# Seven block products for slabs of a feed-forward's first matrices, squares on ScalarE

## The reference

```python
def squared_relu_mlp(x, w1, w2):
    return jnp.square(jax.nn.relu(x @ w1)) @ w2      # w1: 1024 x 4096, w2: 4096 x 1024, DEPTH = 2 layers

for i in range(DEPTH):
    ...                                              # mix = attention (i = 0) or state space (i = 1)
    x = layer_norm(DN_ALPHA * x + mix, ...)
    x = layer_norm(DN_ALPHA * x + squared_relu_mlp(x, mlp_w1[i], mlp_w2[i]), ...)
```

## Time and profile before

| | us |
|---|---|
| median of three runs (lowest, highest) | 2304.91 (2304.09, 2306.13) |
| the profiled execution, whole | 2307.19 |
| its span, first to last instruction | 2305.3 |
| TensorE busy in it | 2272.6 |
| VectorE busy | 979.7 |
| ScalarE busy | 444.2 |
| mean granted TensorE clock, share of full | 0.995 |

### The profile page before, as it was taken

One profiled execution on the slowest core, in us unless ns is written; L12 is line 12 of the kernel. 1 busy time (PEld: TensorE's weight loads), 2 busy tenths in 40 slices (PEclk: granted clock), 3 DMA queues, 4 the chain that ended last, 5 costly groups with the idle time before them and its releaser, 6 DMA issues.

```text
span 2305.3 us, 25572 instructions
## 1 busy us (share of the span) xinstructions
PE 2272.6 (99%) x10790; PEld 1369.9 (59%) x10790; DVE 979.7 (42%) x1950; ACT 444.2 (19%) x1011; POOL 73.9 (3%) x130
## 2 busy tenths in 40 slices
PE   9999999999999999999999999999999999999998
PEld 6568547886487459997434333335999643333332
DVE  3567656667576557653211111125774311111122
ACT  3410003357100011220211111101132121111111
POOL 2000000000100000000000000000000000000000
PEclk9999999999999999999999999999999999999999
DMA  7289625354698415246999999994426599999997
GB/s 292 114 309 403 252 78 204 147 183 180 238 403 328 178 65 197 97 182 256 390 427 427 428 427 428 428 418 185 164 97 247 222 407 428 428 427 428 427 428 286
DMA packets 59167, 671.64 MB, mean 291 GB/s; under 512 B 7504, under 2 KB 7792, under 8 KB 18720
## 3 DMA queue, kind: packets, MB, share of 16 engines
q1 hardware_dynamic: 51888, 649.45, 69.0%
q0 software_dynamic: 7152, 20.43, 2.6%
HBM read 666.59 MB, written 3.26 MB: 291 GB/s over the span
## 4 chain that ended last, share of the span: by engine, by line
PE 87%; DMA 9%; DVE 2%; issue 0%; ACT 0%; SPq 0%; POOL 0%; DVEq 0%; POOLq 0%; ACTq 0%
PE ps L101 85%; DMA ring<-in_exp_w 5%; DMA arena<-in_exp_w 3%; DVE arena L114 1%; PE ps L349 1%; DVE arena L117 1%; PE ps L2753 1%; DMA arena<-ssm_rows 1%; DMA ring<-in_ada_w 0%; PE ps L638 0%; DMA ring<-in_attn_w_in 0%; PE ps L1915 0%; DVE X L117 0%; PE ps L1234 0%; ACT arena L106 0%
## 5 line engine op out<-in xcount | busy, mean ns | idle before, releaser
L101 PE MATMUL ps<-arena 128*64 128x512 f32 (+8 forms) x4036 | 957.3, 466 | 15.1 <-DMA arena<-in_exp_w 6.0
L101 PEld LDWEIGHTS ps<-arena 128*128 128x128 f32 (+2 forms) x4036 | 462.2, 167 | 466.1 <-issue 436.6
L101 PE MATMUL ps<-ring,arena 128*64 128x512 f32 (+2 forms) x1720 | 460.6, 584 | 1.9 <-DMA ring<-in_exp_w 1.9
L101 PE MATMUL ps<-XTGB,ring 128*128 128x256 f32 (+1 forms) x2160 | 423.5, 353 | 0.0
L101 PEld LDWEIGHTS ps<-XTGB,ring 128*128 128x128 f32 x2160 | 367.1, 190 | 52.8 <-issue 10.7
L101 PEld LDWEIGHTS ps<-ring,arena 128*64 128x64 f32 (+1 forms) x1720 | 174.0, 150 | 259.0 <-issue 254.5
L122 DVE COPY arena<-ps 128x512 f32<-128x512 f32 (+5 forms) x133 | 63.3, 496 | 417.4 <-PE ps L101 298.5
L121 ACT COPY arena<-ps 128x512 f32<-128x512 f32 (+3 forms) x179 | 81.6, 475 | 677.9 <-PE ps L2753 285.1
L101 PE MATMUL ps<-XTGB,arena 128*64 128x512 f32 (+2 forms) x736 | 200.7, 428 | 0.0
L105 ACT ACTIVATE arena<-ps 128x512 f32<-128x512 f32 (+2 forms) x95 | 51.2, 545 | 677.1 <-PE ps L101 672.3
L101 PE MATMUL ps<-ring,XTGB 128*128 128x512 f32 (+3 forms) x484 | 169.1, 504 | 2.0 <-DMA ring<-in_attn_w_in 1.9
(11 more groups left out here) (151 smaller groups left out, 950.8 us busy)
## 6 DMA issues: line engine op xcount, KB each, us to landing
arena<-in_exp_w SPq DMA_DIRECT2D x90, 2048.0 KB, 26.6
ring<-in_exp_w SPq DMA_DIRECT2D x68, 2048.0 KB, 28.0
ring<-in_mlp_w SPq DMA_DIRECT2D x25, 2048.0 KB, 9.7
ring<-in_ada_w SPq DMA_DIRECT2D x20, 2048.0 KB, 9.8
XTGB<-in_exp_w SPq DMA_DIRECT2D x18, 2048.0 KB, 32.3
ring<-in_ssm_w_in SPq DMA_DIRECT2D x12, 2048.0 KB, 7.7
ring<-in_w_in SPq DMA_DIRECT2D x12, 2048.0 KB, 8.0
ring<-in_gate_w SPq DMA_DIRECT2D x12, 2048.0 KB, 7.6
```

Of the source, the lines that this page charges most:

```text
L101: return self.e.matmul(o, lhsT=lhsT, rhs=rhs, start=start, stop=stop, skip_group_check=True)
```

## The change

For slabs 2 and 4 of layer 0 and 2, 4 and 6 of layer 1 the product with w1 is made by seven block products instead of eight. `w1_x_sums` makes four sums of blocks of `XT` once a layer on VectorE, `w1_sums` four sums of weight blocks for each such slab (one of them in place in the slab), `w1_products` issues the products (7 x 2 column blocks x 4 chunks, 128 columns each) into four banks, and `w1_results` adds them up from PSUM into `hT` in seven VectorE instructions; ScalarE copies the first product. ScalarE then takes relu and square of the whole slab. For all other slabs of 1 to 7 the square, too, moves from VectorE to ScalarE, right after the relu. VectorE's program in `mlp_dve` is put in a new order, with the sums for slab s + 2 ahead of the pieces of step s and the results of slab s + 1 behind them. `W1_LOADS` and `PIECES` stay as they are. New buffers `hX`, `hS` lie in the arena.

```diff
--- before.py
+++ after.py
@@ -873,6 +873,78 @@
         ORDER = (1, 2, 3, 5, 7, 6, 4), (1, 5, 6, 2, 3, 7, 4)
         PLAIN = {2: 0, 3: 1, 4: 2}
 
+        W1_BLOCKS = (2, 4), (2, 4, 6)
+        W1_GROUPS = ((1, 6), (5, 7), (3, 4), (2,))
+
+        def w1_x_sums(v, l, nn):
+
+            x1, x2, x3, x4 = hX[l]
+            v.wait_ge(at("XT", nn, 0), at("XT", nn, 1))
+            k = v.then_inc(v.tt(x1, XT[:, 0:4, P:T], XT[:, 0:4, 0:P], ALU.subtract), ("hX", l))
+            v.then_inc(v.tt(x3, XT[:, 4:8, P:T], XT[:, 0:4, P:T], ALU.subtract), ("hX", l))
+            v.wait_ge(k)
+            k = v.then_inc(v.tt(x2, XT[:, 4:8, P:T], x1, ALU.subtract), ("hX", l))
+            v.wait_ge(k)
+            v.then_inc(v.tt(x4, XT[:, 4:8, 0:P], x2, ALU.subtract), ("hX", l))
+
+        def w1_sums(v, l, s):
+
+            w = weights(("m1", l, s))
+            s1, s2, s4 = hS[l]
+            v.wait_ge(at("w", ("m1", l, s)), at("hp", l, s - 2, 2) if s > 2 else None)
+            k = v.then_inc(v.tt(s1, w[:, 0:4, T:2 * T], w[:, 4:8, T:2 * T], ALU.add), ("hS", l, s, 5))
+            v.wait_ge(k)
+            k = v.then_inc(v.tt(s2, s1, w[:, 0:4, 0:T], ALU.subtract), ("hS", l, s, 6))
+            v.then_inc(v.tt(w[:, 0:4, T:2 * T], w[:, 0:4, 0:T], w[:, 0:4, T:2 * T], ALU.subtract), ("hS", l, s, 7))
+            v.wait_ge(k)
+            v.then_inc(v.tt(s4, w[:, 4:8, 0:T], s2, ALU.subtract), ("hS", l, s, 3))
+
+        def w1_products(pe, l, s):
+            slab_ = ("m1", l, s)
+            w = weights(slab_)
+            x1, x2, x3, x4 = hX[l]
+            s1, s2, s4 = hS[l]
+            pairs = {1: (XT[:, 0:4, 0:P], w[:, 0:4, 0:T]), 2: (XT[:, 4:8, 0:P], w[:, 4:8, 0:T]), 3: (XT[:, 4:8, P:T], s4),
+                     4: (x4, w[:, 4:8, T:2 * T]), 5: (x1, s1), 6: (x2, s2), 7: (x3, w[:, 0:4, T:2 * T])}
+            pe.wait_ge(at("w", slab_), at("hX", l))
+            for r, group in enumerate(W1_GROUPS):
+                ps = bank(pe, "hp", l, s, r)
+                for n, p in enumerate(group):
+                    x, y = pairs[p]
+                    if p in (3, 5, 6, 7):
+                        pe.wait_ge(at("hS", l, s, p))
+                    for f in range(2):
+                        for c in range(4):
+                            ins = pe.mm(ps[:, n * T + f * P:n * T + (f + 1) * P], y[:, c, f * P:(f + 1) * P], x[:, c, :],
+                                        c == 0, c == 3)
+                pe.then_inc(ins, ("hp", l, s, r), *([("free", slab_)] if r == 3 else []))
+
+        def w1_product(l, s, r, n):
+            return ps_of("hp", l, s, r)[:, n * T:(n + 1) * T].rearrange("p (f t) -> p f t", f=2)
+
+        def w1_parts(hT, s):
+            g = hT[:, 4 * s:4 * s + 4, :]
+            return g[:, 0:2, 0:P], g[:, 0:2, P:T], g[:, 2:4, 0:P], g[:, 2:4, P:T]
+
+        def w1_results(v, l, s, hT):
+            c11, c12, c21, c22 = w1_parts(hT, s)
+
+            def plus(o, r, n, x, *done):
+                return v.then_inc(v.tt(o, w1_product(l, s, r, n), x, ALU.add), ("read", "hp", l, s, r), *done)
+
+            v.wait_ge(at("hp", l, s, 0), at("hP1", l, s))
+            k = plus(c12, 0, 1, c11)
+            v.wait_ge(k, at("hp", l, s, 1))
+            k = plus(c21, 1, 1, c12)
+            e = plus(c12, 1, 0, c12)
+            v.wait_ge(k)
+            k = plus(c22, 1, 0, c21, ("hsum", l, s))
+            v.wait_ge(k, e, at("hp", l, s, 2))
+            plus(c12, 2, 0, c12, ("hsum", l, s))
+            plus(c21, 2, 1, c21, ("hsum", l, s))
+            v.wait_ge(at("hp", l, s, 3))
+            plus(c11, 3, 0, c11, ("hsum", l, s))
+
         def blocks_a(hT, s):
             return [hT[:, 4 * s + 2 * k:4 * s + 2 * k + 2, t * P:(t + 1) * P] for t in range(2) for k in range(2)]
 
@@ -914,7 +986,10 @@
                                 mid=None if t else lambda: turn_rows(pe, n, 1, X, at("x", n, 1)))
                 else:
                     ada_pe(pe, l, s, acc)
-                    gemm_f(pe, ("m1", l, s), ("m1", l, s), 4, mid=(lambda: ada_pe(pe, l, 8, acc)) if s == 7 else None)
+                    if s in W1_BLOCKS[l]:
+                        w1_products(pe, l, s)
+                    else:
+                        gemm_f(pe, ("m1", l, s), ("m1", l, s), 4, mid=(lambda: ada_pe(pe, l, 8, acc)) if s == 7 else None)
                 if s == 1:
                     for t in range(2):
                         turn(pe, ("h0", l), t, lambda c: h0[:, t, c * P:(c + 1) * P], 4, at("relu 0", l, t))
@@ -965,10 +1040,21 @@
                 act.then_inc(act.act(h0[:, t, :], ps_of("m1", l, 0, t), ACT.Relu), ("relu 0", l, t),
                              ("read", "m1", l, 0, t))
             for s in range(1, 8):
+                if s in W1_BLOCKS[l]:
+                    act.wait_ge(at("hp", l, s, 0))
+                    act.then_inc(act.cp(w1_parts(hT, s)[0], w1_product(l, s, 0, 0)), ("hP1", l, s), ("read", "hp", l, s, 0))
+                    h = hT[:, 4 * s:4 * s + 4, :]
+                    act.wait_ge(at("hsum", l, s))
+                    k = act.then_inc(act.act(h, h, ACT.Relu))
+                    act.wait_ge(k)
+                    act.then_inc(act.act(h, h, ACT.Square), ("h", l, s))
+                    continue
                 for fp in range(2):
+                    h = hT[:, 4 * s + 2 * fp:4 * s + 2 * fp + 2, :]
                     act.wait_ge(at("m1", l, s, fp))
-                    act.then_inc(act.act(hT[:, 4 * s + 2 * fp:4 * s + 2 * fp + 2, :], two(ps_of("m1", l, s, fp)),
-                                         ACT.Relu), ("relu", l, s, fp), ("read", "m1", l, s, fp))
+                    k = act.then_inc(act.act(h, two(ps_of("m1", l, s, fp)), ACT.Relu), ("read", "m1", l, s, fp))
+                    act.wait_ge(k)
+                    act.then_inc(act.act(h, h, ACT.Square), ("h", l, s))
                 if s == 1:
                     for t in range(2):
                         act.wait_ge(at("h0", l, t, 0))
@@ -1040,18 +1126,18 @@
                 norm_v(v, n, 1, rest)
 
         def mlp_dve(v, l, hT, acc, ab, sA, sB):
+            w1_x_sums(v, l, 1 + 2 * l)
             for s in range(8):
-                if s == 7:
-                    ada_dve(v, l, s, acc, ab)
-                    block_sums(v, l, 0, hT, sA, sB)
-                for fp in range(2 if s else 0):
-                    h = hT[:, 4 * s + 2 * fp:4 * s + 2 * fp + 2, :]
-                    v.wait_ge(at("relu", l, s, fp))
-                    v.then_inc(v.tt(h, h, h, ALU.mult), ("h", l, s))
-                if s < 7:
-                    if l and s == 1:
-                        gain_dve(v, 0)
-                    ada_dve(v, l, s, acc, ab)
+                if l and s == 1:
+                    gain_dve(v, 0)
+                if s and s + 2 in W1_BLOCKS[l]:
+                    w1_sums(v, l, s + 2)
+                ada_dve(v, l, s, acc, ab)
+                if s == 0:
+                    w1_sums(v, l, 2)
+                if s + 1 in W1_BLOCKS[l]:
+                    w1_results(v, l, s + 1, hT)
+            block_sums(v, l, 0, hT, sA, sB)
             for s in range(1, NS):
                 block_sums(v, l, s, hT, sA, sB)
 
@@ -1072,6 +1158,9 @@
         h00 = arena.get(2, 512)
         sU0 = arena.get(512)
         sA0, sB0 = strassen_places(acc_at, h0_at, ab_at)
+        hX, hS = [None, None], [None, None]
+        hX[0] = [arena.get(4, P) for _ in range(4)]
+        hS[0] = [arena.get(4, T) for _ in range(3)]
 
 
 
@@ -1556,6 +1645,11 @@
         sU1 = arena.get(512)
         assert arena.pos <= TOP + SLAB
         sA1, sB1 = strassen_places(acc_at, h0_at, ab_at)
+        arena.pos = xbase
+        hX[1] = [arena.get(4, P) for _ in range(4)]
+        arena.pos = TOP + 2 * SLAB
+        hS[1] = [arena.get(4, T) for _ in range(3)]
+        assert arena.pos <= ASZ - D
         rs2 = small[:, 60:62]
 
 
```

## The result

The changed kernel takes 2312.59 us (median of 9 runs, 2310.33 to 2317.60) against 2306.13 us before (9 runs, 2304.09 to 2310.33): a ratio of 1.0033, 95% interval 1.0024 to 1.0041, 5.5 to 9.5 us slower. The profiled execution (2317.60 us, span 2315.8) was the slowest of the nine, and it must be read with that in mind.

What follows compares the result with a forecast made beforehand. Bound by both TensorE's slabs and VectorE with the ring, it put layer 0 at +1.7 + 1.4 = +3.1 and layer 1 at -1.2 + 1.4 = +0.2, together +3.3 us on 2304.91: 2308.2 us, range 2302.5 to 2313.

Steps and rivals of the forecast that it cites:

- rival 2: Slower by the ring: delayed loads of pieces 6 and 7 meet others; together +7.5 us, 2312.4 us; chance 0.30.
- the rule for loads: In the ring, a load lands at the later of issue + 7.6 us and the load before + 4.9 us.
- The bound: Before slab 5, TensorE's slabs and VectorE with the ring are chains of equal length; TensorE waits only 0.24 us.
- TensorE's gain: Seven block products take 12.51 us a slab instead of 13.8: 1.3 us saved a slab, 6.4 us in all.
- Rival 4: Slower by TensorE: weight loads bind the short passes, at worst +52 us over five slabs, 2357 us; chance 0.03.
- Squares at nothing: Squares moved to ScalarE, 0.62 us per 128x512 operation, fall in idle time between relus and count as nothing.
- VectorE's added durations: Four sums of XT 2.7 us; per Strassen slab, sums 4.7 and additions 2.7 us; layer 0 17.5, layer 1 24.9 us.
- Layer 0, walked: TensorE idles 4.1 to 5.3 us before slab 5 for piece 7; selector matmuls 1.1 to 2.3 us later, middle +1.7.
- Layer 1, walked: Idle 2.2 to 3.4 us before slab 5; selector matmuls -0.5 to +0.7, middle +0.1; slab 6 saves 1.28; layer -1.2 us.
- The clock: TensorE's clock falls behind each of the two new waits, costing 1.4 us each, bounds 0 and 2.
- Rival 3: The waits before slab 5 come but the clock holds: +0.5 us, 2305.4 us; chance 0.17.
- rival 1: All hidden: pieces arrive before TensorE needs them, so 6.4 us are saved, 2298.5 us; chance 0.12.

Runs made afterwards that it cites:

- e2: Changed kernel with the second group of selector matmuls (pieces 4 to 7) one slab later, before slab 6: 0.9969 of the time before the change, 2298.87 us.
- e1: Changed kernel without any slab by block products; squares stay on ScalarE, VectorE's order is the new one: ratio 0.9997 to before the change, 2305.83 us.
- e3: Changed kernel with VectorE's sums for slab 4 (and 6) behind the two pieces of their step, not ahead: ratio 0.9997 to before the change, 2305.11 us.
- e11: The changed kernel run once more, unchanged: ratio 1.0032 to before the change, 2312.75 us.
- e6: Changed kernel with block products in layer 1 alone (slabs 2, 4 and 6): ratio 1.0002 to before the change, 2307.95 us.
- e4: Changed kernel with idle matmuls filling TensorE's wait ahead of the second group of selector matmuls: ratio 1.0012 to before the change, 2308.13 us.

## Why the prediction was wrong, point by point

Forecast were 2308.2 us and most likely no change; measured were 2312.6 and a loss clear of noise. The time lies near the upper end of the range, at rival 2 (2312.4). The mechanism was right. The step that failed is the size of two terms of the sum: the rule for loads, which let piece 7 come too early (some 1.6 us in layer 0, 0.4 to 1.6 in layer 1), and the price of the slow clock, 1.4 us a wait, which was 1.7 to 3.0. Another 1.2 us of the distance to 2312.6 is the kernel before itself, 2306.13 us by nine runs where the forecast started from 2304.91.

- **The bound.** Right. Two chains of equal length met before slab 5, and the change lengthened VectorE's.
- **TensorE's gain**, 1.3 us a slab, 6.4 in all. Right: 12.5 us a slab in the trace, and e2 brings it to the end, 7.1 us (4.8 to 9.7). Rival 4 is out. The estimate from the Trainium skill ("TensorE: Matmul & The Clock Gate", section "Back-to-back issue gap"), 2.8 us lost a slab, is out too: the trace shows 111.7 ns at 128 columns and a slab 1.3 us shorter. (Its 6.3 us for 64 long passes goes with the columns; halfway between the two figures, as the text has it, would be 6.8 us.)
- **Squares at nothing.** Right (e1).
- **VectorE's added durations.** Right to 0.1 us.
- **Layer 0, walked: +1.7.** The order of waits was right (piece 3, the sums for slab 4, piece 6), the size not. This profile runs 0.67 us later from its start on, so 202.30 becomes 202.97; the selector matmuls came at 206.26, +3.3 us. What failed is the rule for loads. The load of slab 4 was issued at 162.07 and took 12.65 us, where the walk has 11.8 (161.5 to 173.3); that of piece 6, "issue + 7.6", took 8.84, at the upper end of the 7.6 to 8.8 that I carried. These two stand one behind the other on the path. Of the 6.15 us idle I had 4.1 to 5.3. All nine traces with block products in layer 0 agree on slab 4's load, 12.6 to 13.1 us, and eight on piece 6's, 8.4 to 8.8 us; in e3, where it is issued behind others, it took 10.4.
- **Layer 1, walked: selector matmuls +0.1.** Same step. Against its own start of slab 2 (650.93) the trace has them 1.7 us later; in e11 1.4, and in e6, where they start at 686.11 from 642.89, 0.5 us, which is within the walk's -0.5 to +0.7. Slab 4's load took 12.9 us (12.7 in e6 and e11; 11.6 walked) and piece 7's 8.7 (7.6 in e6; 7.6 walked).
- **The clock: 1.4 us each.** Right in kind (e4), too low in size. In layer 0 it was 1.8 us, and 2.2 in e11. In layer 1 it was 0.85 on the selector matmuls and 2.1 on slab 5, 3.0 us, and 1.7 in both e6 and e11. The nearest row was a wait of 2.76 us, while the waits had become 3 to 6 us long. The 2 us that I kept as a bound were the better price.
- **The sum.** +3.1 for layer 0 became +5.1, +0.2 for layer 1 became +1.8 to +3.4. Together 6.9 to 8.5; the medians, 2306.13 and 2312.59, say 6.5.
- **The rivals.** Rival 2 is what happened by its time, but not by its mechanism or its sign. It let the loads of pieces 6 and 7 meet others and land over 9 us after issue; in layer 0 they took 8.8 and 7.8 us, and piece 7's in layer 1 8.7. (Layer 1's piece 6 took 10.1, but nothing waited for it.) The delay came instead from two places, slab 4's load and a smaller excess at piece 6's or 7's, so that its 2312.4 is in part luck. I had written that it decides from 0.6 us more delay in each layer; with so small a distance, 0.30 for it and 0.41 for any slower result were too low. Rival 3 (the clock holds) is refuted, rival 1 too.

What stays open: why slab 4's load, issued with others in flight, lands 0.8 to 1.3 us later than the distance between landings says (in layer 0 in nine traces, in layer 1 in the three compared), and why a load with none ahead takes 7.6 us in one place or execution and 8.7 in another. No run was made on either cause.

## What to carry to other kernels

Before taking work off the bounding engine, ask which other engine delivers to it just in time: here TensorE's one wait was 0.24 us long, and the 2.6 us saved ahead of it in layer 0 became waiting, with the delay of VectorE's added work and the clock's loss on top. If the result that is waited for has a user with slack, as the selector matmuls had, move the place where it is asked for: one condition turned 1.0033 into 0.9969. Price a new wait of 3 to 6 us on TensorE at its length and some 2 us more: the slow clock behind such waits cost 1.4 to 3.0 us here.

## What the runs showed of the hardware that was not expected

- TensorE stood 5 us among eight transposes, waiting for nothing that the profile shows, in the same place in both profiled executions of one kernel (5.07 and 4.98 us), and not in the one of the kernel with 32 more matmul instructions ahead. A difference of up to 5 us between two kernels of this length may be no more than that, so that a total alone doesn't size an edit of a few microseconds; its own stretch does.
- The slow clock's cost doesn't follow the length of the wait. A wait of 2.10 us already cost 1.7 us behind it (e3, layer 0), as much as one of 6.15 us did in layer 0 after the change (1.8 us). One of 2.38 us in the same execution cost nothing (e3, layer 1, granted clock 1.00), and one of 4.29 us cost 3.0.
